# Spreading rows between projection halves, a third early slot, and the second latent layer's first modulation group behind the first expert's gate weights

## The chip, the cores and the metric

One core of one Trainium2 chip runs the kernel; the other cores stand idle. The metric is the device time of one execution in microseconds (us). All arithmetic is float32. Every weight is read once from HBM, 661 MB in all, so two things can set the pace: the rate at which the 16 DMA engines bring weights in, and TensorE (PE), which multiplies them.

## What is computed

Two models follow each other on 256 tokens of width 1024. The first block modulates the normed input (`mod = c @ w_ada + b_ada`), projects it, mixes it by an mLSTM and by a Hyena convolution, projects back, and runs an expert-choice mixture of 16 experts. The second model has two layers. Each of them has its own modulation, mixes the 256 latent tokens and (in layer 0) 256 context tokens by neighbourhood attention, gated linear attention and grouped attention, and ends in a SwiGLU. Cut to what matters here:

```python
def reference(x, c, w_ada, ..., c_2, ctx_2, c_ctx_2, w_ada_2, ...):
    # first block
    mod = (c @ w_ada[0] + b_ada[0])[:, None, :]          # six parts of 1024
    h = rms_norm(x, g_mix) * (1 + sc1) + sh1
    q, k, v, o, gates, hx = jnp.split(h @ w_in + b_in, split_pts, axis=-1)
    x = x + gt1 * (concatenate([mlstm(q, k, v, o, gates), hyena(hx)]) @ w_out)
    hf = rms_norm(x, g_ffn) * (1 + sc2) + sh2
    x = x + gt2 * expert_choice_moe(hf, w_router, w_gate, w_up, w_down)
    x = rms_norm(x, g_final)
    # second model, layers l = 0, 1
    for l in range(2):
        mod, mod_c = silu(c_2) @ w_ada_2[l] + b_ada_2[l], silu(c_ctx_2) @ w_ada_2[l] + b_ada_2[l]
        ...  # mixers, w_out, SwiGLU for latent tokens, and for the context where l == 0
```

The modulation products (`c @ w_ada`) depend on no token. The kernel can therefore place them anywhere before their first use, and the change moves four of them.

## The kernel before, in words

**The weight stream.** Nearly all weights are cut into slots of up to 4096 float32 columns on 128 partitions (2 MiB, "2048 KB" in the profile). The list `stream` holds them in the order in which PE takes them, and SyncE (SP) issues one DMA for each in just that order (`load`, L3110 to L3114). Most slots land in `ring`, which has room for four full slots (16384 columns). A few, named in `early` (L588), land in stretches of `arena` that are dead at that time. Before each DMA, SP waits until PE has finished with the slot `after[n]`, which lay in the same place, or eight slots earlier. SP is in order: while it waits for one slot, all later ones wait too.

**Order of the stream around the change.** After the mixers' projections (z, x1, q, x2, v, o, k) come `out0`, `out1`, then `ada0_7` to `ada0_11` and `ada1_0` to `ada1_3`, and from `n_before` on the experts: `gate0_0` to `gate0_3`, `up0_0` to `up0_3`, and so on, with slots of context weights between them. `ada0_j` are the twelve slots of the modulation of latent layer 0; `ada1_0` to `ada1_3` are the first group of layer 1. Two slots are early ones, `ada0_9` and `ada0_10`. `gate0_0` and `gate0_1` are early ones too; they lie at arena columns 16424 and 20520, and SP waits for `h_ready` 2 (normed tokens of the experts, told by VectorE after L2167) before them.

**Modulation steps.** The list `ADA` gives the steps of the modulation, and `ada(n)` takes the next n of them on PE, ScalarE (ACT) and VectorE (DVE) alike. A "rows" step multiplies one slot (16 matmuls at L1284); four of them fill one PSUM bank, ACT copies it to `row_stage`, and a "turn" step transposes it to columns (8 matmuls in the profile at L1301), which DVE adds to the bias (L1905, L1900). In the kernel before, `ada0_7` to `ada0_10` are taken after the mixers' output (L1551), `ada0_11` after the transposes of the normed tokens (L1564), and `ada(5)` at L1569 takes `ada1_0` to `ada1_3`, with the turns of the groups `ada0_2` and `ada1_0`, while DVE picks the best tokens of each expert (L2186 to L2192).

**Into the experts.** PE then spreads the choice (L1573), gathers the chosen tokens of the first four experts (`tokens_of(0)`, L1583), multiplies the gate slots of expert 0 (L1616), gathers the tokens of the other twelve (`other_tokens`, L1589 to L1599), and goes on with `up0`. ACT copies each gathered bank out. When all of them are copied, SP loads the tables of the second model (L3153 to L3155). From here on, stages of the context's computation stand between the experts' slots.

**The first mixers.** PE projects `x2` in two halves (L1265 by way of `project`), then `token_rows(1, ...)` spreads columns over banks with 16 transposes (L1402), of which DVE takes maxima (L2050 to L2053), then `z_spectrum(0)` (L1418) opens the bank that DVE frees after those maxima (L1900), since banks 0 to 6 are taken in rotation.

## Time and profile before

| | |
|---|---|
| median of 3 runs | 2242.75 us (2240.03 to 2244.28) |
| profiled execution | 2238.4 us, of which the span is 2236.6 us |
| PE busy, loads of weights busy | 1999.5 us (89%), 1406.8 us (63%) |
| DVE, ACT, POOL busy | 588.9, 423.1, 206.4 us |
| DMA | 664.24 MB, mean 297 GB/s |
| mean granted clock of TensorE | 0.964 of full speed |

The profiled execution is 4.35 us shorter than the median. The page's strip of 40 slices (each 55.9 us) shows where each resource is loaded:

```profile
PE   8989998976888898987888887999999999999997
DMA  9938799999999999999999999531587742044450
GB/s 366 374 144 350 297 424 405 422 425 427 389 415 426 427 425 424 422 420 426 425 424 427 419 380 365 138 114 39 180 297 218 187 141 101 15 151 151 127 155 19
```

Each digit is the busy share of a slice in tenths. The first five slices are the mixers of the first block, the sixth to the twenty-fifth hold the experts and the context, and the rest holds the two latent layers.

### The profile page before, as it was taken

How to read it: one execution, taken by the hardware profiler on the slowest of the kernel's cores; microseconds unless marked ns; L12 is line 12 of the kernel's file. 1: busy time of each engine (PE TensorE's matmuls, PEld its weight loads, DVE VectorE, ACT ScalarE, POOL GpSimd, SP SyncE). 2: the span in 40 equal slices, each digit the busy share in tenths (PEclk: the TensorE clock that was granted, in tenths of full speed). 3: DMA queues.
4: the chain of work that ended last, by engine and by line, in shares of the span. 5: the costliest groups of instructions: out<-in, count | busy, mean ns of one | idle time of the engine just before them, and what ended most of it. 6: DMA issues, size and time to landing. Idle time of an engine off the chain costs nothing.

```text
span 2236.6 us, 32618 instructions
## 1 busy us (share of the span) xinstructions
PE 1999.5 (89%) x14110; PEld 1406.8 (63%) x14110; DVE 588.9 (26%) x1168; ACT 423.1 (19%) x776; POOL 206.4 (9%) x183
## 2 busy tenths in 40 slices
PE   8989998976888898987888887999999999999997
PEld 4857575632455466653565543756888877588886
DVE  5655410114412000000002101454432034640001
ACT  3222221211312000000001211434200033630001
POOL 0830000001000000000000000325000003700000
PEclk9999999998998999999999899999999999999999
DMA  9938799999999999999999999531587742044450
GB/s 366 374 144 350 297 424 405 422 425 427 389 415 426 427 425 424 422 420 426 425 424 427 419 380 365 138 114 39 180 297 218 187 141 101 15 151 151 127 155 19
DMA packets 181382, 664.24 MB, mean 297 GB/s; under 512 B 17431, under 2 KB 121400, under 8 KB 142648
## 3 DMA queue, kind: packets, MB, share of 16 engines
q1 hardware_dynamic: 181240, 662.15, 75.7%
q8 instruction: 112, 1.84, 0.3%
q14 instruction: 30, 0.25, 0.0%
HBM read 661.08 MB, written 1.05 MB: 296 GB/s over the span
## 4 chain that ended last, share of the span: by engine, by line
PE 46%; DMA 22%; DVE 4%; ACT 4%; issue 1%; POOL 0%; SPq 0%; ACTq 0%; DVEq 0%; POOLq 0%
PE ps L1177 19%; PE ps L679 9%; DMA ring<-in_context_weights 8%; DMA ring<-in_w_gate 7%; DMA ring<-in_w_down_slots 4%; PE ps L1616 4%; DMA ring<-in_w_up 3%; PE ps L1642 2%; PE ps L1013 2%; PE ps L1186 2%; PE ps L980 2%; ACT arena L2546 1%; PE ps L875 1%; PE ps L705 1%; PE ps L1089 1%
## 5 line engine op out<-in xcount | busy, mean ns | idle before, releaser
L1177 PE MATMUL ps<-arena,ring 128*128 128x256 f32 x1984 | 429.9, 379 | 1.0 <-DVEq L391 0.9
L1177 PEld LDWEIGHTS ps<-arena,ring 128*128 128x128 f32 x1984 | 376.5, 190 | 54.2 <-issue 1.7
L1616 PE MATMUL ps<-ring,arena 128*32 128x256 f32 x4032 | 264.0, 409 | 80.0 <-DMA ring<-in_w_gate 43.7
L679 PE MATMUL ps<-arena,ring 128*128 128x256 f32 (+2 forms) x1372 | 309.7, 386 | 8.6 <-DMA ring<-in_context_weights 8.6
L679 PEld LDWEIGHTS ps<-arena,ring 128*128 128x128 f32 (+2 forms) x1372 | 249.5, 187 | 74.1 <-DMA ring<-in_context_weights 24.4
L1616 PEld LDWEIGHTS ps<-ring,arena 128*32 128x32 f32 x4032 | 127.9, 116 | 200.7 <-DMA ring<-in_w_gate 51.3
L2253 ACT ACTIVATE arena<-ps 128x512 f32<-128x512 f32 (+3 forms) x143 | 76.7, 536 | 738.2 <-PE ps L679 327.8
L1642 PE MATMUL ps<-ring,arena 128*32 128x512 f32 x1024 | 139.1, 668 | 61.1 <-DMA ring<-in_w_down_slots 54.3
L1642 PEld LDWEIGHTS ps<-ring,arena 128*32 128x32 f32 x1024 | 29.8, 117 | 153.0 <-DMA ring<-in_w_down_slots 90.5
L3059 POOL TENSOR_TENSOR XC<-XC,arena 128x256 f32<-128x256 f32 x32 | 23.4, 731 | 989.2 <-ACT XC L2347 968.9
L3069 POOL TENSOR_SCALAR arena<-arena 128x512 f32<-128x512 f32 x48 | 78.4, 1634 | 88.0 <-DVE arena L2964 84.7
L679 PE MATMUL ps<-ring,arena 128*128 128x256 f32 (+3 forms) x312 | 85.7, 426 | 0.0
L1265 PE MATMUL ps<-arena,ring 128*128 128x256 f32 x384 | 84.2, 380 | 1.4 <-ACTq L391 1.4
L2718 DVE SCALAR_TENSOR_TENSOR XC<-ps,arena,XC 128x256 f32<-128x256 f32 x48 | 23.2, 484 | 225.7 <-PE ps L1177 144.2
L980 PE MATMUL ps<-arena,ring 128*128 128x256 f32 x352 | 78.6, 381 | 4.4 <-DMA ring<-in_context_weights 4.4
L1265 PEld LDWEIGHTS ps<-arena,ring 128*128 128x128 f32 x384 | 72.6, 190 | 12.7 <-DVEq L391 2.2
L1873 ACT ACTIVATE arena<-ps 128x256 f32<-128x256 f32 x32 | 12.3, 384 | 352.8 <-PE ps L1616 352.6
L980 PEld LDWEIGHTS ps<-arena,ring 128*128 128x128 f32 x352 | 66.2, 190 | 19.1 <-DMA ring<-in_context_weights 8.9
L679 PEld LDWEIGHTS ps<-ring,arena 128*128 128x128 f32 x312 | 54.5, 190 | 26.9 <-issue 17.1
L3013 DVE TENSOR_TENSOR arena<-arena,ps 128x512 f32<-128x512 f32 x20 | 13.8, 688 | 212.3 <-PE ps L1177 212.3
L2222 DVE TENSOR_TENSOR arena<-arena,ps 128x256 f32<-128x256 f32 x32 | 13.5, 421 | 210.8 <-ACT arena L1873 209.6
L1013 PE MATMUL ps<-arena,ring 128*128 128x258 f32 x224 | 51.0, 381 | 0.0
(374 smaller groups left out, 2015.0 us busy)
## 6 DMA issues: line engine op xcount, KB each, us to landing
ring<-in_w_up SPq DMA_DIRECT2D x64, 2048.0 KB, 13.2
ring<-in_w_down_slots SPq DMA_DIRECT2D x64, 2048.0 KB, 14.2
ring<-in_w_gate SPq DMA_DIRECT2D x62, 2048.0 KB, 13.9
ring<-in_w_ada SPq DMA_DIRECT2D x28, 2048.0 KB, 9.4
ring<-in_w_ffn_in SPq DMA_DIRECT2D x44, 1024.0 KB, 7.7
ring<-in_context_weights SPq DMA_DIRECT2D x35, 1024.0 KB, 14.6
ring<-in_w_ffn_out SPq DMA_DIRECT2D x16, 1408.0 KB, 7.0
ring<-in_w_in SPq DMA_DIRECT2D x9, 2048.0 KB, 11.2
```

Source lines behind the costliest of these rows:

```text
L679: m = mm(o, a, x, start=(k == 0 and r == 0), stop=(k == kt - 1 and last))
L980: m = mm(b[i][:, T * x:T * x + T], w[:, k % 2, c:c + P], HID[:, k, :], start=(k == 0 and x == 0), stop=(k == 21 and x == 1))
L1013: m = mm(b[:, 0:RAW], w[:, k, c:c + P], raw[:, k, :], start=(k == 0), stop=(k == KD - 1))
L1177: m = mm(b, w[:, k, c:c + P], src[:, k, :], start=(k == 0), stop=(k == kt - 1))
L1186: m = mm(b[:, 0:T], held["w"][:, k, c:c + P], oT[X][:, k, :], start=(k == 0), stop=(k == KD - 1))
L1265: m = mm(b[:, T * i:T * i + T], w[:, k, P * (j + i):P * (j + i) + P], src(k), start=(k == 0), stop=(k == ktiles - 1))
L1616: m = mm(b[u][32 * c:32 * c + 32, T * x:T * x + T], xs[:, 2 * h + k, CAP * e:CAP * e + CAP], w[:, k, at_:at_ + T], start=(h == 0 and k == ...
L1642: m = mm(b[a][64 * n + 32 * j:64 * n + 32 * j + 32, :], hdT[:, 2 * a + j, ch, :], w[:, j, at_:at_ + W], start=(i == 0 and odd == 0), stop= ...
L2253: step(a(dst, src, f, **kw), frees=name if frees else None)
L2718: step(stt(out=x, in0=b[:, o:o + T], scalar=mod2[:, l, gate + m, st:st + 1], in1=x, op0=ALU.mult, op1=ALU.add), frees=name if last else None)
L3059: step(nc.gpsimd.tensor_tensor(hat[st][n % 2][:, x, :], ex[st][n % 2][:, x, :], glqk[:, x, :], ALU.mult), lev_ready if x else None)
L3069: step(nc.gpsimd.tensor_scalar(Pr[n % 8], Pr[n % 8], sm[:, n % 8:n % 8 + 1], None, ALU.mult), pn_ready[X])
```

## The change

It has three parts. First, `project("x2")` gets a callback: `token_rows(1, "arow")` is now issued between the two halves of the x2 projection and no longer behind them. Second, `ada0_11` becomes an early slot at arena columns 16424 to 20520, where queries, keys and two of the convolved thirds are dead after the mLSTM weights are made (`p_ready` 1); SP waits for that. Because `gate0_0` lands in the same columns, SP now also waits before `gate0_0` until PE has finished with `ada0_11` (`freed[in_queries]`). Third, `ada1_0` to `ada1_3` leave their place ahead of `n_before` and stand behind `gate0_3` in the stream. PE takes them (`ada(4)`) behind the second half of expert 0's gate, ahead of `other_tokens`, and turns them behind it. ACT and DVE take their steps at matching places.

```diff
--- before.py
+++ after.py
@@ -468,7 +468,7 @@
         for n, count in (("z", 0), ("x1", 0), ("q", 0), ("x2", 1), ("v", 1), ("o", 3), ("k", 4)):
             stream += [(n, cols(w_in, column[n], 512))] + ada_tiles[at_tile:at_tile + count]
             at_tile += count
-        stream += [(f"out{j}", cols(w_out, 512 * j, 512)) for j in range(2)] + ada_tiles[at_tile:]
+        stream += [(f"out{j}", cols(w_out, 512 * j, 512)) for j in range(2)] + ada_tiles[at_tile:24]
 
         SUMMED = 12
         row_buffer = [i % 3 for i in range(SUMMED)]
@@ -557,6 +557,8 @@
                 e = i // 2
                 w = I["w_" + kind][0, e].rearrange("(h p s) n -> p h s n", p=P, s=2)
                 stream += [(f"{kind}{e}_{h}", w[:, h]) for h in (2 * (i % 2), 2 * (i % 2) + 1)]
+            if s == 1:
+                stream += ada_tiles[24:]
             if s in CTX_AT:
                 stream += CTX_STAGES[CTX_AT[s]][1]
         n_moe = len(stream)
@@ -585,8 +587,10 @@
         NU, NP = len(UNITS2), len(HEADS2)
 
 
-        early = {n_before: 16424, n_before + 1: 20520, n_before + 6: 12312}
-        early |= {n: {"ada0_9": 5120, "ada0_10": 0}[name] for n, (name, _) in enumerate(stream) if name in ("ada0_9", "ada0_10")}
+        early = {n_before: 16424, n_before + 1: 20520, n_before + 10: 12312}
+        dead = {"ada0_9": 5120, "ada0_10": 0, "ada0_11": 16424}
+        early |= {n: dead[name] for n, (name, _) in enumerate(stream) if name in dead}
+        in_queries = [name for name, _ in stream].index("ada0_11")
         landing, count = [], [0] * LANES
         place_of, after = [], []
         top = 0
@@ -618,10 +622,10 @@
         ADA = [[("rows", "ada", j)] for j in range(4)] + [[("turn", "ada", 0)], [("sum", "ada", 1)], [("turn", "ada", 1)], [("sum", "ada", 2)]]
         ADA += [[("rows", "ada", 10)], [("rows", "ada", 11)]]
         ADA_GROUPS = [("ada", j) for j in range(3)] + [("ada0_", j) for j in range(3)] + [("ada1_", 0)]
-        for g in range(3, 7):
+        for g in range(3, 6):
             name, j = ADA_GROUPS[g]
             ADA += [[("rows", name, 4 * j), ("turn", *ADA_GROUPS[g - 1])]] + [[("rows", name, 4 * j + h)] for h in range(1, 4)]
-        ADA += [[("turn", "ada1_", 0)]]
+        ADA += [[("turn", "ada0_", 2)]] + [[("rows", "ada1_", h)] for h in range(4)] + [[("turn", "ada1_", 0)]]
         LATE = {n: name for n, (name, _) in enumerate(stream) if name[:4] == "late"}
         late_sum, late_row = at(24064, 2048), at(26112, W)
         GROUP = {"ada": 0, "ada0_": 3, "ada1_": 6}
@@ -1296,7 +1300,7 @@
                 n = 1 if name == "ada" else 2
                 turned[0] += 1
                 pe.wait_ge(row_ready, turned[0])
-                b = open_bank(pe, f"col_{name}{j}", MIX_BANKS)
+                b = open_bank(pe, f"col_{name}{j}", CTX_BANKS if name == "ada1_" else MIX_BANKS)
                 for i in range(4):
                     m = mm(b[:, 4 * n * i:4 * n * i + 4 * n], stage_of(name, j)[:, P * i:P * i + P], tb("pick")[:, 0:8:3 - n], start=True, stop=True)
                 close_bank(m, f"col_{name}{j}")
@@ -1369,10 +1373,12 @@
             T1v = T1.rearrange("p (a b) -> p a b", b=T)
 
 
-            def project(n):
+            def project(n, between=None):
                 w = take(n)
                 for i in range(2):
                     fmajor(f"{n}{i}", w, 2 * i, lambda k: hT[:, k, :])
+                    if i == 0 and between is not None:
+                        between()
                 release_with(f"{n}1")
 
             def by_groups(name, w):
@@ -1452,8 +1458,7 @@
             close_bank(m, "F")
             z_by_token(0)
             ada()
-            project("x2")
-            token_rows(1, "arow")
+            project("x2", between=lambda: token_rows(1, "arow"))
             z_spectrum(0)
             ada(2)
             w = take("v")
@@ -1566,7 +1571,7 @@
             for t in range(TT):
                 m = nc.tensor.transpose(b[0:NE, P * t:P * t + P], aff[:, t, :], ident)
             close_bank(m, "affT")
-            ada(5)
+            ada()
             pe.wait_ge(best_ready, 1)
             for i in range(2):
                 b = open_bank(pe, f"best{i}", MIX_BANKS)
@@ -1665,7 +1670,9 @@
                         gu = [open_bank(pe, f"gu{e}{u}", EXPERT_BANKS) for u in range(2)]
                     expert("gate", i, gu)
                     if i == 1:
+                        ada(4)
                         other_tokens()
+                        ada()
                     if g and i % UNITS < 4:
                         combine(g - 1, i % UNITS, TURN_BANKS)
                 elif kind == "up":
@@ -1852,7 +1859,7 @@
                     b = read_bank(act, f"ht{t}{half}")
                     step(a(htok[:, t, 512 * half:512 * half + 512], b[:], ACT.Copy), frees=f"ht{t}{half}")
                     tell(ht_ready)
-            ada(6)
+            ada(2)
             def tokens_of(g):
                 for half in range(2):
                     b = read_bank(act, f"xs{g}{half}")
@@ -1860,6 +1867,7 @@
                     tell(xs_ready)
 
             tokens_of(0)
+            ada(4)
             for g in range(1, GROUPS):
                 tokens_of(g)
             for g2 in range(2):
@@ -2191,7 +2199,7 @@
             for i in range(2):
                 step(tt(own[e16, i, :].rearrange("p (e s) -> p e s", s=CAP), bc(best[e16, i, :], 1, NE, CAP), bc(ident[e16, 0:NE], 2, NE, CAP), ALU.mult))
             tell(best_ready)
-            ada(5)
+            ada()
             which = read_bank(dve, "best0")
             for t in range(TT):
                 step(ts(sel[:, t].rearrange("p e s -> p (e s)"), which[:], tb("token")[:, t:t + 1], None, ALU.is_equal), frees="best0" if t else None)
@@ -2209,6 +2217,7 @@
                     if sem:
                         tell(sem)
 
+            ada(5)
             dve.wait_ge(s_x, 32)
             dve.wait_ge(xs_ready, 8)
             dve.wait_ge(ct_ready, 2)
@@ -3137,6 +3146,8 @@
                     sp.wait_ge(y_ready, 2)
                 if stream[n][0] == "ada0_10":
                     read_bank(sp, "num111")
+                if stream[n][0] == "ada0_11":
+                    sp.wait_ge(p_ready, 1)
                 load(n)
                 for i in rows_behind.get(stream[n][0], ()):
                     load_row(i)
@@ -3145,9 +3156,10 @@
             for n in range(n_before, len(stream)):
                 if n == n_before:
                     sp.wait_ge(h_ready, 2)
-                if n == n_before + 6:
+                    sp.wait_ge(*freed[in_queries])
+                if n == n_before + 10:
                     sp.wait_ge(ht_ready, 4)
-                if n == n_before + 9:
+                if n == n_before + 13:
                     sp.wait_ge(xs_ready, 8)
                     sp.wait_ge(ct_ready, 2)
                     sp.dma_start(arena[:, 0:n_tab2], I["tables2"]).then_inc(s_tab2, 16)
```

## Rows read from the trace of the kernel before

**Rows 1.** Windows: stretch, length, busy us by engine, PEclk, DMA share, GB/s.
```profile
0.00:260.00 260.00, 243.98 (x1206) 167.58 (x1210) 150.51 (x262) 66.55 (x117) 66.77 (x65) 0.97 0.78 301
260.00:400.00 140.00, 123.26 (x1138) 82.06 (x1130) 19.23 (x55) 27.38 (x45) 0.00 (x0) 0.93 0.99 410
400.00:540.00 140.00, 110.00 (x1351) 62.02 (x1348) 31.47 (x68) 26.44 (x42) 11.81 (x16) 0.94 1.00 423
...
1580.00:1810.00 230.00, 229.88 (x1078) 200.47 (x1077) 61.22 (x73) 20.69 (x35) 3.65 (x5) 1.00 0.72 224
```

**Rows 2.** Waits of PE from 300 to 600 us: total, times, longest.
```profile
PE ps L1616 <- DMA ring<-in_w_gate: 10.4, 6, 3.8
```

**Rows 3.** Timeline of SP's queue: start, length, line, what it issues.
```profile
209.47 3.11 SPq L3114 DMA_DIRECT2D ring<-in_w_ada  x2
212.70 7.03 SPq L3114 DMA_DIRECT2D arena<-in_w_ada  x2
241.46 24.92 SPq L3114 DMA_DIRECT2D ring<-in_w_ada  x5
266.43 0.47 SPq L3144 DMA_DIRECT2D XC<-in_ctxT  x1
266.99 3.58 SPq L3114 DMA_DIRECT2D arena<-in_w_gate  x2
...
313.09 0.33 SPq L3153 DMA_DIRECT2D arena<-in_tables  x1
```

**Rows 4.** Windows in the front and of two gaps among the experts, columns as before.
```profile
230.00:240.00 10.00, 10.00 (x48) 8.79 (x48) 1.32 (x3) 0.63 (x1) 0.00 (x0) 1.00 0.14 57
241.00:244.80 3.80, 3.80 (x20) 3.33 (x19) 0.97 (x2) 0.63 (x1) 0.00 (x0) 1.00 0.62 183
244.80:316.60 71.80, 64.80 (x577) 42.97 (x576) 20.09 (x54) 20.69 (x36) 0.00 (x0) 0.93 0.97 396
600.00:610.00 10.00, 9.54 (x84) 5.48 (x84) 2.59 (x6) 2.34 (x7) 0.00 (x0) 0.83 0.80 301
1300.00:1320.00 20.00, 20.00 (x117) 10.06 (x112) 1.75 (x1) 0.47 (x1) 0.00 (x0) 0.91 0.82 315
```

**Rows 5.** Timeline of PE in the first mixers, with idle time and its releaser.
```profile
94.10 14.06 PE L1265 MATMUL ps<-arena,ring 128*128 128x256 f32 x64
108.00 1.91 PE L1402 MATMUL ps<-tab,arena 128*128 128x128 f32 x16
117.99 5.95 PE L1418 MATMUL ps<-arena,tab 128*128 128x512 f32 x8 [8.08 <-DVE arena L1900]
...
172.34 3.70 PE L1418 MATMUL ps<-arena,tab 128*128 128x512 f32 x8
```

**Rows 6.** Timeline of DVE around them, and its writing of the normed tokens.
```profile
98.53 5.28 DVE L1986 SCALAR_TENSOR_TENSOR arena<-arena,par 128x2048 f32<-128x2048 f32 x2
108.70 0.69 DVE L2050 TENSOR_REDUCE arena<-ps 128x4 f32<-128x512 f32 x1 [4.89 <-PE ps L1402]
117.67 0.17 DVE L1900 TENSOR_TENSOR arena<-ps,par 128x16 f32<-128x16 f32 x1
...
254.31 4.13 DVE L2167 SCALAR_TENSOR_TENSOR arena<-XC,arena 128x256 f32<-128x256 f32 x8
```

**Rows 7.** Timeline of PE from the slot ada0_11 to the first up slots.
```profile
264.03 1.92 PE L1284 MATMUL ps<-ring,arena 128*32 128x512 f32 x16
...
283.77 6.72 PE L1583 MATMUL ps<-arena 128*128 128x128 f32 x32 [0.95 <-issue]
291.22 3.66 PE L1616 MATMUL ps<-arena 128*32 128x256 f32 x64 [0.73 <-issue]
...
299.33 11.57 PE L1583 MATMUL ps<-arena 128*128 128x128 f32 x96
310.74 1.04 PE L1598 MATMUL ps<-tab,arena 128*128 128x128 f32 x8
311.71 3.66 PE L1616 MATMUL ps<-ring,arena 128*32 128x256 f32 x64
```

## Prediction, made before the changed kernel was run

> **What bounds the kernel now.** I read the windows first, because the bound changes by stage. Up to 260 us PE is busy 244 of 260 us and DMA has holes (share 0.78). From 260 us on DMA is full: its share is 0.99 to 400 us and 1.00 with 423 GB/s to 540 us, while PE idles 30 us of 140. In the latent layers PE is busy 229.88 of 230 us [rows 1]. The page's strip shows the same nine tenths or more up to about 1370 us. PE waits for gate slots there, for instance 10.4 us in six places [rows 2]. So the experts' stretch ends when a fixed number of bytes has arrived, and nothing in it can be made up by PE. An idle us of DMA ahead of that stretch moves the end by one us; an idle us of PE there costs something only if it delays a DMA. I therefore read next what SP issued and when [rows 3], and the windows beside it.
>
> The reader is to see one hole. `ada0_7` to `ada0_10` are issued from 209.47 to 219.7 us; the next issue is at 241.46 us [rows 3]. In between the DMA share falls to 0.14 [rows 4]. The issue at 241.46 is `ada0_11`, which waits for the ring place of `out0`. Behind it everything flows: `ada1_0` to `ada1_3`, the last at about 266.0 us when PE ends `ada0_11` (264.03 + 1.92) [rows 7], then the context tokens at 266.43 and `gate0_0` at 266.99 [rows 3].
>
> **A clock for DMA.** A full slot is 2.097 MB, 4.96 us at 423 GB/s [rows 1]. The windows give 183 x 3.8 = 0.70 MB to 244.8 us and 396 x 71.8 = 28.43 MB from there to 316.6 us, 29.13 MB in all [rows 4]. That is just five modulation slots, four gate and four up slots (13 x 2.097 = 27.26 MB), the context tokens (1.05) and one context slot of 1600 columns (0.82). So before the change `up0_3` has fully arrived at 316.6 us, and it is my mark, since the bytes behind it are the same in both kernels. The 0.70 MB are 1.64 us of full rate, so the flow starts in effect at 244.8 - 1.64 = 243.2 us, 1.7 us after its issue at 241.46. At full rate the rest would take 67.2 us; it took 71.8. Those 4.6 us are small holes, one of them around the late last slot at 266 us.
>
> **Part 1, rows between the halves of x2.** It removes nothing; 16 transposes move. PE now does 7.0 us of x2 from 94.10 (half of 14.06), the transposes (1.91) to 103.1, and the second half to 110.1 us [rows 5]. DVE's row sums end at 98.53 + 5.28 = 103.81 us; it then waited 4.89 us for the transposes [rows 6]. Now it starts at 103.9. From its first maximum to the end of L1900 it needs 117.84 - 108.70 = 9.1 us [rows 6], so the bank is free at 113.0 and not 117.9. `z_spectrum` starts at 113.1 and not 117.99: **4.9 us gained**, and of 8.08 us of idle PE about 3.0 stay [rows 5]. The slot of x2 is freed 2 us later (110.1), so `o` is issued 2 us later; it is taken over 30 us on, which hides it. Could the gain be larger? `z_spectrum` took 5.95 us after the 8 us of idle and 3.70 us in its second use [rows 5], so up to 2.25 us more come back if the clock stays up over a pause of 3 us. I take none of it and keep it as a bound. Could it be nothing? If ACT or POOL were late next, yes; PE idles nowhere else for them up to 218 us, so I keep 0 only as the other bound. The transfers up to `ada0_10` are each issued on an event of PE or DVE, so they shift by the same 4.9 us.
>
> **Part 2, the early slot.** `ada0_11` no longer waits for `out0` but for `p_ready` 1, which PE's numerators wait for as well, and `ada0_10` ahead of it waits for the last numerator. So it is issued right behind `ada0_10`, at 219.7 - 4.9 = 214.8 us, and the context tokens behind it. This fills the hole with 4.96 + 2.48 = 7.4 us of work for DMA. In exchange `gate0_0` waits until PE has ended `ada0_11`. PE takes that slot at the same place in its program, so this is 265.95 - 4.9 = **261.05 us**. `h_ready` 2 is out by 254.31 + 4.13 - 4.9 = 253.5 [rows 6] and not the last. All else that SP could load, `gate0_1` to `gate0_3` and the rest, is queued behind this wait, though ring places come free from `out1` on. DMA has nothing from about 234 us (the four slots ended near 232 before [rows 4], so 227 now, plus 7.4) to 262.8. The hole grows from 11 us to 28.
>
> **Part 3, layer 1's group moved.** The four slots, 19.8 us of DMA time, were what DMA did from 246 to 266 us, in a stretch where gates could not be loaded; now they stand behind the gates, in the full stretch. The four "rows" steps (4 x 1.92 = 7.7 us) and a turn (about 1.05) leave PE ahead of the gates and come in behind them. Best tokens are then waited for by PE for DVE alone, as before. PE goes from `ada0_11` at 261.0 to `tokens_of(0)` at about 272, to `gate0_0` at about 280 instead of 291.2 [rows 7]. That gain is not kept: `ada1_3` is the eighth slot after the wait and lands at 262.8 + 8 x 4.96 = 302.5, or some 303.3 with its completion. Its rows end at 305.2, `other_tokens` (11.57 + 1.04) at 317.8, the turn at 318.9. `up0_0` then starts 7.2 us later than the 311.71 of before [rows 7]. The tables were issued 1.3 us after the last transposes [rows 3, 7], now at 319.1, while DMA still has slots to bring; no new hole there. The bank of the turn comes from the context's four and the rotation moves by one; each is freed by an ACT copy of 0.6 us, and I cost that at nothing.
>
> **The sum.** From the wait to my mark are 4 gates, 4 modulation and 4 up slots and the context slot, 12 x 2.097 + 0.82 = 25.98 MB, 61.4 us at 423 GB/s. They start in effect at 261.05 + 1.7 = 262.8 and end at 324.2 us, against 316.6: **+7.6 us**. Behind the mark I worked the ring places out by the rule of `after`: 31 slots, the last in the second group's down part, wait for another slot than before, mostly by one place, some earlier and some later; I cost that at nothing while DMA is full, and the gaps' loss bounds it. PE waits for DMA in both, so the delay stays to the end of the experts, and the latent layers have the same work. The profiled execution would be 2238.4 + 7.6 = 2246.0; the median, 4.35 us above it, 2242.75 + 7.6 = **2250.4 us**. Bounds: 2.25 less by the clock (+5.3), 4.6 more if the new flow has as many small holes as the old (+12.2), 4.9 more if part 1 gives nothing (+12.5; both together +17.1).
>
> One price differs by page. The row says 423 GB/s [rows 1]. The Trainium skill, page "DMA: Bandwidth & Descriptors", section Specifications, gives an HBM limit of about 358 GB/s per core. By that the 25.98 MB would take 72.6 us, an estimate, and the delay would be larger by some 11 us; the trace does not agree, with 423 GB/s over 140 us, and it decides.
>
> **Rivals.**
> *The delay is taken up on the way* (within 0.2%). DMA has gaps among the experts, 301 GB/s from 600 to 610 us (2.9 us lost) and 315 from 1300 to 1320 us (5.1 us lost) [rows 4]. If those gaps came from a computation that runs on its own time, a later stream would fill them, and 7.6 - 2.9 - 5.1 is about 0: 2242 to 2246. For it: PE is busy 9.54 of 10 and 20 of 20 us there [rows 4]. Against it: ahead of these places PE waits for slots, so its work there is late by as much as the slots.
>
> *PE, not DMA, sets the pace up to 540 us* (the other side, faster). A full DMA could merely be running ahead. Then PE has `up0_0` at: `gate0_0` 279.7, gates 7.7, rows 7.7, gather 12.6, turn 1.05, that is 308.8, 2.9 us earlier than 311.71 [rows 7]; with the 2.25 us of clock it gains 5.2 us, 2237.6. It decides if every slot behind the gates has landed when PE asks. Against it stand the 10.4 us of waits for gates [rows 2] and PE's 30 idle us of 140 [rows 1]. The Trainium skill, page "Perfetto Trace Analysis", section Optimization Strategy, says that a kernel whose most-contended engine changes over time may gain by interleaving the regimes; by that rule PE work moved from the mixers into the DMA-bound experts should pay, which is this rival. The rows agree that there are two regimes, but the bytes moved with the work.
>
> *Part 1 does not do what it says*: a second wait (POOL's convolution, or the bank of the second half) holds PE until 118. Then the wait for `ada0_11` ends at 265.95 and the sum is +12.5, 2255.3. Against it: nothing but DVE releases PE in that place [rows 5].
>
> **How the numbers follow.** A measurement of this kernel tells about 0.2% (4.5 us) from no change. The forecast, held gates with +5.3 to +9.5 (2248.0 to 2252.3), gets 0.48; more holes or no gain in part 1 (+9.5 to +17, to 2259.8) 0.20; the delay taken up (2239 to 2247) 0.20; faster 0.12. Slower is then 0.48 + 0.20 = 0.68 (all but a sliver of these lie above 2247.2), less 0.01 for that sliver: 0.67; within 0.2% 0.21; faster 0.12. The range must leave out no more than 0.2: from 2239.0, which leaves out most of the faster case (0.11), to 2257.0, which cuts the top of the holes' case (0.05).
>
> **What would show it.** In the trace after: PE's idle ahead of L1418 about 3 us, its start at about 113; the issue of `ada0_11` near 215 us; no issue of SP from about 216 to 261 us, with a DMA share near nothing from 235 to 261; `gate0_0` at 261; `gate0_0` multiplied near 280, `ada1_3` not before 303; full DMA behind it and each later issue about 7 to 8 us later, up to the last down slots. I am wrong if SP issues a gate slot before 255 us, if DMA in the later gaps loses clearly less than before, or if the start of `up0_0` is earlier than 311.7.

## The result, and the profile after

The changed kernel takes 2254.18 us (median of 4 runs, 2252.07 to 2257.05) against 2241.39 us (4 runs) of the kernel before: 12.8 us more, ratio 1.006 with a 95% interval of 1.0043 to 1.0077. I had forecast 2250.4 us, slower, with a range of 2239 to 2257. Direction and range held. The cost is 5 us larger than the sum's 7.6; the time is only 3.8 us above the forecast, because the kernel before measured 1.4 us less than the median that I had added the sum to.

The profiled execution has a span of 2250.3 us, 13.7 us above the 2236.6 of before. First, SP's queue in the changed kernel (start, length, line, what it issues):

```profile
206.63 7.54 SPq L3123 DMA_DIRECT2D arena<-in_w_ada  x3
214.23 0.46 SPq L3155 DMA_DIRECT2D XC<-in_ctxT  x1
259.98 0.82 SPq L3123 DMA_DIRECT2D arena<-in_w_gate  x2
260.85 1.15 SPq L3123 DMA_DIRECT2D ring<-in_w_gate  x2
262.04 24.11 SPq L3123 DMA_DIRECT2D ring<-in_w_ada  x4
...
320.72 0.33 SPq L3165 DMA_DIRECT2D arena<-in_tables  x1
```

Where before had an issue at 241.46 and a full queue behind it [rows 3], nothing is issued here from 214.7 to 259.98 us. Then four gate slots go out within 2 us; the places of the two ring slots among them had been free since PE ended the products with `out0` (e5 below issues into that place at 235.25 us) and with `out1` (at about 242.3 us in this trace). The windows of the same stretch (columns as in rows 1) show what DMA does meanwhile:

```profile
220.00:230.00 10.00, 10.00 (x52) 8.78 (x51) 3.21 (x9) 0.00 (x0) 0.00 (x0) 1.00 1.02 424
230.00:240.00 10.00, 10.00 (x48) 8.79 (x47) 2.90 (x6) 1.26 (x2) 0.00 (x0) 1.00 0.40 137
240.00:250.00 10.00, 9.19 (x59) 5.62 (x57) 4.54 (x8) 3.47 (x7) 0.00 (x0) 1.00 0.00 1
250.00:260.00 10.00, 9.88 (x96) 4.98 (x92) 3.51 (x13) 5.33 (x10) 0.00 (x0) 1.00 0.01 2
260.00:270.00 10.00, 3.99 (x12) 2.71 (x13) 7.49 (x25) 2.48 (x5) 0.00 (x0) 0.62 0.92 357
```

PE's timeline from the first mixers and from the gates on:

```profile
101.37 1.91 PE L1408 MATMUL ps<-tab,arena 128*128 128x128 f32 x16
103.11 7.07 PE L1269 MATMUL ps<-arena,ring 128*128 128x256 f32 x32
112.75 5.12 PE L1424 MATMUL ps<-arena,tab 128*128 128x512 f32 x8 [2.56 <-DVE arena L1908]
...
278.61 3.66 PE L1621 MATMUL ps<-arena 128*32 128x256 f32 x64 [0.69 <-ACT arena L1866]
282.09 3.64 PE L1621 MATMUL ps<-ring,arena 128*32 128x256 f32 x64
288.37 1.92 PE L1288 MATMUL ps<-ring,arena 128*32 128x512 f32 x16 [2.65 <-DMA ring<-in_w_ada]
293.35 3.50 PE L1288 MATMUL ps<-ring,arena 128*32 128x512 f32 x16 [3.06 <-DMA ring<-in_w_ada]
298.30 1.92 PE L1288 MATMUL ps<-ring,arena 128*32 128x512 f32 x16 [1.45 <-DMA ring<-in_w_ada]
303.48 3.56 PE L1288 MATMUL ps<-ring,arena 128*32 128x512 f32 x16 [3.26 <-DMA ring<-in_w_ada]
306.97 11.57 PE L1588 MATMUL ps<-arena 128*128 128x128 f32 x96
...
320.14 3.66 PE L1621 MATMUL ps<-ring,arena 128*32 128x256 f32 x64
```

The first spectrum (L1424) starts at 112.75 us instead of 117.99 [rows 5]. PE reaches the first gate slot 12.6 us earlier than before and `up0_0` 8.4 us later [rows 7], with 10.4 us of waiting for the four modulation slots in between.

**The lag by bytes.** To follow it to the end I summed the rates of the windows of 10 us from 0 on and read off when each kernel had moved the same number of MB. 101.3 MB are the mark of the prediction: in the kernel before they are reached at 316.7 us. As the end of the experts I take the start of the last combination on PE (16 matmuls at L1655, L1660 after the change).

```
                 101.3 MB   125 MB   220 MB   end of experts   span
before             316.7     372.6    600.7      1380.4       2236.6
changed kernel     322.7     381.4    610.9      1390.4       2250.3
lag                 +6.0      +8.8    +10.2        +9.9        +13.7
```

So the lag has three parts: 6.0 us are there at the mark, 4 us arise behind it among the experts, and 3.7 us in the latent layers. Of the last part 3.5 us arise in one place, the start of layer 1. There PE computes the gate ranks (16 matmuls). PE's timeline in the kernel before:

```profile
1817.92 3.65 PE L1013 MATMUL ps<-arena,ring 128*128 128x258 f32 x16
1821.86 4.96 PE L700 MATMUL ps<-arena,ring 128*32 128x256 f32 x16 [0.29 <-ACT arena L2256]
1827.53 7.17 PE L705 MATMUL ps<-arena,ring 128*128 128x256 f32 x32 [0.70 <-DVE arena L2752]
```

and DVE's, the row that frees the bank of the second raw query:

```profile
1827.12 0.36 DVE L2752 TENSOR_SCALAR arena<-arena,ps 128x256 f32<-128x256 f32 x1
```

The same place in the changed kernel, PE:

```profile
1828.14 3.65 PE L1017 MATMUL ps<-arena,ring 128*128 128x258 f32 x16
1837.80 1.93 PE L704 MATMUL ps<-arena,ring 128*32 128x256 f32 x16 [6.00 <-DVE arena L2761]
1839.66 8.72 PE L709 MATMUL ps<-arena,ring 128*128 128x256 f32 x32
```

and DVE:

```profile
1837.34 0.36 DVE L2761 TENSOR_SCALAR arena<-arena,ps 128x256 f32<-128x256 f32 x1
```

The two DVE rows are 10.22 us apart, like the rows of PE ahead of them. Before, PE did not need that bank and had followed ACT's tiles one by one from 1821.86 on. Now it stands until 1837.34 + 0.36 = 1837.70 and starts at 1837.80. That is 5.7 us more of lag. The product then takes 1.93 us instead of 4.96, since it no longer follows ACT, and the wait of 0.70 us behind it is gone, which gives 3.8 us back. The next product takes 8.72 instead of 7.17 us, with a mean granted clock of 0.82 from 1839.6 to 1848.3 us and of 1.00 in the same place before, 1.55 us more. Together the lag grows from 10.2 to 13.7 us. The order in which banks are opened says why: in the kernel before `gl_lrx1` opens bank 7, in the changed one bank 4, which `rq1x1`, the second raw query, holds. The latent layers share one rotation over banks 4 to 7 with the context, and the moved turn of `ada1_0` takes one place in it. In layer 0 the gate ranks move from bank 4 to bank 5 by the same step; the wait there is 4.93 us instead of 4.03.

### The profile page after: what moved, and what is told of

Read it like the earlier page. It is cut to its first block, busy times and chain, and to the rows that moved or that the text cites. A ratio compares the mean times of both kernels' runs of the same rounds, so it can differ in the third digit from the quotient of the medians.

```text
span 2250.3 us, 32619 instructions
## 1 busy us (share of the span) xinstructions
PE 2004.7 (89%) x14110; PEld 1407.0 (63%) x14110; DVE 591.4 (26%) x1168; ACT 423.1 (19%) x776; POOL 206.4 (9%) x183
## 4 chain that ended last, share of the span: by engine, by line
PE 47%; DMA 22%; DVE 4%; ACT 3%; issue 1%; ACTq 0%; POOL 0%; SPq 0%; DVEq 0%; POOLq 0%
PE ps L1181 19%; PE ps L683 10%; DMA ring<-in_w_gate 7%; DMA ring<-in_w_down_slots 6%; DMA ring<-in_context_weights 5%; PE ps L1621 4%; DMA ring<-in_w_up 4%; PE ps L1647 2%; PE ps L1017 2%; PE ps L1190 2%; PE ps L984 2%; ACT arena L2555 1%; PE ps L879 1%; PE ps L709 1%; PE ps L845 1%
## 5 line engine op out<-in xcount | busy, mean ns | idle before, releaser
L1647 PE MATMUL ps<-ring,arena 128*32 128x512 f32 x1024 | 141.9, 683 | 59.0 <-DMA ring<-in_w_down_slots 53.0
L1288 PE MATMUL ps<-ring,arena 128*32 128x512 f32 x304 | 42.5, 689 | 13.4 <-DMA ring<-in_w_ada 12.6
## 6 DMA issues: line engine op xcount, KB each, us to landing
ring<-in_w_gate SPq DMA_DIRECT2D x62, 2048.0 KB, 13.3
```

The costliest lines, as they stand in the source:

```text
L1288: m = mm(row_bank[0][32 * g:32 * g + 32, :], cpad[:, 2 * h + k, :], w[:, k, W * g:W * g + W], start=(h == 0 and k == 0), stop=(h == 3 and ...
L1647: m = mm(b[a][64 * n + 32 * j:64 * n + 32 * j + 32, :], hdT[:, 2 * a + j, ch, :], w[:, j, at_:at_ + W], start=(i == 0 and odd == 0), stop= ...
```

## The experiments

Theory H: an empty DMA queue costs its length, since DMA is full from there to the end of the experts; the wait of `gate0_0` for `ada0_11` empties it. Theory B: the 3.5 us at layer 1 are the shifted rotation of banks. Rivals: part 3 costs by PE's late start of `up0_0`; the slot in the dead columns costs by itself; there is slack behind the front.

**e1_rows_alone**, the kernel before with part 1 only:

```diff
-            project("x2")
-            token_rows(1, "arow")
+            project("x2", between=lambda: token_rows(1, "arow"))
```

> The kernel before with the first part alone: the transposes of the first maxima stand between the halves of the x2 projection. In the changed kernel PE's first spectrum started at 112.75 instead of 117.99 us and took 5.12 instead of 5.95, and everything on PE up to 240 us came 6.07 us earlier. Theory (the gain of part 1 is real and reaches the end, since it shifts the start of the full DMA stretch): each issue from 120 us on about 6 us earlier, the last down slots as well, total 6 us less than before (ratio 0.997). Rival (what ends the experts does not hang on the front): the front 6 us earlier and the total within 1 us of before.

Measured: 2235.1 us (11 runs) against 2240.84, ratio 0.9976 (0.9965 to 0.9988). The mark is reached at 310.6 us, 6.1 earlier than in the kernel before; the experts end at 1376.4 us, 4.1 earlier in this profile, and the median is 5.7 us lower. Part 1 is a gain of 4 to 6 us that reaches the end, and the rival of slack falls.

**e2_rows_behind**, the changed kernel with the same lines undone.

> The changed kernel with its first part undone. Theory: the wait of gate0_0 for the slot ada0_11 ends at about 266 instead of 259.98 us, all later issues are 6 us later than in the changed kernel, and the total is some 6 us above it, 19 us above before (ratio 1.0085). Rival (the first part costs or gives nothing at the end): the changed kernel's time, ratio 1.006.

Measured: 2262.17 us (4 runs), ratio 1.0092 (1.0074 to 1.011), 8.0 us above the changed kernel's median. `gate0_0` was issued at 264.13 us and the mark reached at 326.9, each 4.2 later than in the changed kernel. I had expected 266 us and 6 us. The direction follows the theory, the size is not settled: the profiled span, 2253.7 us, is only 3.4 us above the changed kernel's, while the medians of 4 runs each are 8.0 apart.

**e3_group_ahead**, parts 1 and 2 without part 3:

```diff
         stream += [(f"out{j}", cols(w_out, 512 * j, 512)) for j in range(2)] + ada_tiles[at_tile:]
...
-        early |= {n: {"ada0_9": 5120, "ada0_10": 0}[name] for n, (name, _) in enumerate(stream) if name in ("ada0_9", "ada0_10")}
+        dead = {"ada0_9": 5120, "ada0_10": 0, "ada0_11": 16424}
+        early |= {n: dead[name] for n, (name, _) in enumerate(stream) if name in dead}
...
                     sp.wait_ge(h_ready, 2)
+                    sp.wait_ge(*freed[in_queries])
```

> Parts 1 and 2 without part 3: rows between the halves, ada0_11 early in the dead columns, gate0_0 still waits for it, but ada1_0 to ada1_3 stay ahead of the gates and can fill the time of that wait from the ring. Theory (what costs is an empty DMA queue between 235 and 260 us, not the wait as such): ada1_0 to ada1_3 are issued at about 235.4, 242, 248 and 250 us, gate0_0 at 260, up0_3 has arrived at about 303 instead of 322.7, then DMA has some 5 us of nothing until the chosen tokens are copied and the tables may be loaded at about 308; total 7 to 12 us below before (ratio 0.995 to 0.997). Rival (the early slot itself, with the wait in front of gate0_0, costs): the total above that of the first part alone, ratio near 1.000.

Measured: 2232.27 us (5 runs), ratio 0.9957 (0.9942 to 0.9973): 8.6 us below before and the fastest of all. The hold of `gate0_0` is in this kernel too, but SP has something to issue ahead of it:

```profile
205.85 7.54 SPq L3117 DMA_DIRECT2D arena<-in_w_ada  x3
234.61 15.33 SPq L3117 DMA_DIRECT2D ring<-in_w_ada  x4
249.99 0.47 SPq L3149 DMA_DIRECT2D XC<-in_ctxT  x1
259.19 0.82 SPq L3117 DMA_DIRECT2D arena<-in_w_gate  x2
```

and DMA is full through the hold (windows, last columns DMA share and GB/s):

```profile
245.00:250.00 5.00, 4.19 (x37) 1.33 (x33) 4.16 (x6) 2.96 (x6) 0.00 (x0) 1.00 1.00 392
250.00:255.00 5.00, 5.00 (x54) 2.01 (x54) 1.82 (x6) 2.17 (x5) 0.00 (x0) 1.00 1.02 424
255.00:260.00 5.00, 4.48 (x38) 2.52 (x38) 1.18 (x7) 3.07 (x5) 0.00 (x0) 1.00 1.00 399
...
300.00:305.00 5.00, 5.00 (x62) 4.14 (x65) 0.28 (x2) 2.39 (x4) 0.00 (x0) 1.00 0.54 229
305.00:310.00 5.00, 5.00 (x51) 3.41 (x44) 0.07 (x1) 4.60 (x8) 0.00 (x0) 1.00 0.88 285
```

The mark is reached at 304.3 us. As expected some gain is given back right behind it, where DMA is at 229 and 285 GB/s because the tables wait for the copied tokens (issued at 304.62). So the early slot and the wait are no cost by themselves: with them this kernel is even 2.8 us below e1, which has part 1 alone (2235.1 us).

**e5_no_hold**, parts 1 and 3 without part 2 (`ada0_11` back in the ring, no wait of `gate0_0` for it):

```diff
-        dead = {"ada0_9": 5120, "ada0_10": 0, "ada0_11": 16424}
+        dead = {"ada0_9": 5120, "ada0_10": 0}
...
                     sp.wait_ge(h_ready, 2)
-                    sp.wait_ge(*freed[in_queries])
```

> Parts 1 and 3 without part 2: ada0_11 lands in the ring again behind out0, so gate0_0 waits for the normed tokens only and not for PE's use of ada0_11. Theory (the hold of gate0_0 costs its length): gate0_0 is issued at about 252.4 instead of 259.98 us, up0_3 has arrived at about 315.5 instead of 322.7, the total is 7 us below the changed kernel, 5 to 6 us above before (the shift of banks is still in; ratio 1.0025). Rival (the four modulation slots behind the gates cost, whatever the wait): still 2254, ratio 1.006.

Measured: 2247.05 us (11 runs), ratio 1.0033 (1.0021 to 1.0045), 7.1 below the changed kernel's median. SP's queue, and a window of 5 us:

```profile
235.25 0.37 SPq L3122 DMA_DIRECT2D ring<-in_w_ada  x1
...
252.30 0.82 SPq L3122 DMA_DIRECT2D arena<-in_w_gate  x2
```

```profile
245.00:250.00 5.00, 4.19 (x35) 1.09 (x33) 3.56 (x5) 2.36 (x5) 0.00 (x0) 1.00 0.01 3
```

It stays slower than before although part 1 is in it, since DMA still had nothing to do from 245 us to the issue at 252.30. The mark comes at 317.8 us, 4.9 earlier than in the changed kernel and not 7.2 as expected. Part of the difference lies from 280 to 290 us: DMA moved 311 and then 339 GB/s in windows of 5 us, some 2.3 us of full rate lost, while SP waited for PE to free places in the ring.

Four kernels with part 1 in them now separate the other two parts (medians in us):

```
                     part 2 out          part 2 in
part 3 out     e1    2235.10       e3    2232.27
part 3 in      e5    2247.05       after 2254.18
```

Part 3 costs 12 us by itself and 22 us beside the hold; the hold costs nothing where the four modulation slots stand ahead of it, and 7 us where they do not. Each figure is good to some 3 us; by the ratios, each to the kernel before as measured beside it, they are 13, 23, none and 6. So the cost is not the hold alone. Part 3 took away what the queue could issue (an empty stretch of some 7 us is left even in e5, and the banks of theory B add theirs), and part 2 made the empty stretch longer.

**e9_taken_early** and **e10_longer_hold** change the length of the hold. In e9 PE takes `ada0_11` before the logits, which also makes the logits later:

```diff
             close_bank(m, "ss1")
-            ada(4)
+            ada(5)
...
                     close_bank(m, f"ht{t}{half}")
-            ada()
```

> The changed kernel, and PE takes ada0_11 right behind ada0_10, ahead of the logits: the hold of gate0_0 ends at about 256.5 instead of 259.98 us. Theory (each us of hold is a us at the end, for DMA has nothing from 235 on): gate0_0 issued 3.1 to 3.8 us earlier, total some 3 us less than the changed kernel, about 2251, ratio 1.0045. Rival (the hold is not what costs): unchanged, 1.006.

and in e10 SP waits longer:

```diff
                     sp.wait_ge(*freed[in_queries])
+                    sp.wait_ge(best_ready, 1)
```

> The changed kernel, and SP waits ahead of gate0_0 also until the best tokens are chosen (DVE tells it at 268.2 us in the changed kernel), 8.3 us longer. Theory (each us of hold is a us at the end): total about 8 us above the changed kernel, 2262, ratio 1.0095. Rival (some slack lies between the gates' arrival and the end of the experts, since PE multiplies the first gate slot only at 278.6 us): the gates would land at 276 and be taken nearly as before; total within 3 us of the changed kernel, ratio 1.006 to 1.0075.

Measured: e9 2252.18 us (6 runs), ratio 1.005 (1.0033 to 1.0066), a step in the expected direction that its interval does not separate from the changed kernel; e10 2262.48 us (6 runs), ratio 1.009 (1.0073 to 1.0108), 8.3 us above it, as theory H has it. In one table, by the issue of `gate0_0` in each profile (in e2 and e5 it is not the hold alone that differs: the whole front is later in e2, and e5 has no hold):

```
kernel            gate0_0 issued   mark    end of experts   ratio to before
e5_no_hold            252.30      317.8       1384.8          1.0033
e9_taken_early        256.78      319.9       1388.0          1.005
changed kernel        259.98      322.7       1390.4          1.006
e2_rows_behind        264.13      326.9       1391.7          1.0092
e10_longer_hold       268.39      331.1       1397.4          1.009
```

An issue 16.1 us later moves the mark by 13.3 us and the end of the experts by 12.5 us. From the changed kernel to e10 it is one to one at the mark (8.4 and 8.4 us, 7.0 at the end of the experts); from e5 to the changed kernel 7.7 us of delay are 4.9 at the mark. In e9 PE multiplies the first gate slot at 281.31 us, 2.7 later than in the changed kernel, and the experts end 2.4 us earlier all the same. In e10 the gates came so late that PE waited for them (a row of PE's timeline there), which the changed kernel's PE did not:

```profile
287.10 3.64 PE L1621 MATMUL ps<-ring,arena 128*32 128x256 f32 x32 [3.81 <-DMA ring<-in_w_gate]
```

but the hold had its price already below that point. There it is the stream that is late, not the gate.

**e6_tokens_first**, the changed kernel with the other tokens gathered ahead of the four modulation slots (ACT's copies in the same order):

```diff
                     if i == 1:
-                        ada(4)
                         other_tokens()
+                        ada(4)
                         ada()
```

> The changed kernel, but PE gathers the tokens of the other twelve experts ahead of ada1_0 to ada1_3 and not behind them, so that it does not stand idle for those slots (10.4 us of waits in four places) with 11.6 us of gathering still to do. Theory (DMA sets the pace, and the late gathering costs only the small holes between 320 and 350 us): up0_0 at about 307 instead of 320.14, tables issued at about 301, the loss of those holes, 2 to 3 us, comes back, total 2251 to 2252. Rival (PE's late start of up0_0 is the cost of the change): the total 8 us or more below the changed kernel, 2246 or less.

Measured: 2252.56 us (6 runs), ratio 1.0046 (1.0033 to 1.0059). The tables went out at 308.32 and PE was ready for `up0_0` at 309.6, but it had to wait for the slot:

```profile
300.76 7.07 PE L1288 MATMUL ps<-ring,arena 128*32 128x512 f32 x64 [1.33 <-ACT arena L1873]
308.59 1.06 PE L1305 MATMUL ps<-tab,arena 128*128 128x8 f32 x8 [0.75 <-ACTq L391]
312.36 3.20 PE L1621 MATMUL ps<-ring,arena 128*32 128x256 f32 x32 [2.71 <-DMA ring<-in_w_up]
```

PE could have started `up0_0` 10.5 us earlier than in the changed kernel and did so 7.8 us earlier, and the median fell by 1.6 us, less than the intervals tell apart. I had expected `up0_0` at 307 and the tables at 301. The rival in its full size, that PE's late start is the cost (8 us or more), falls. But the order also has a price: the ring places are freed later, `up0_0` is issued at 302.74 instead of 290.35, and the mark comes at 326.3 us, 3.6 later than in the changed kernel. A smaller gain by PE's earlier start could hide behind that; e6 does not exclude it.

**e4_latent_banks** sets the rotation back where the latent layers begin, **e7_all_banks** right behind the moved turn:

```diff
                 N, bk = f"x{l}", MAIN_BANKS
+                if l == 0:
+                    turn_of[MAIN_BANKS] -= 1
```

```diff
                 close_bank(m, f"col_{name}{j}")
+                if name == "ada1_":
+                    turn_of[CTX_BANKS] -= 1
```

> The changed kernel, with the rotation over PSUM banks 4 to 7 set back by one where latent layer 0 begins, so that the latent layers use the banks of the kernel before; nothing else differs. In the changed kernel the first projection of layer 1 (16 matmuls of the gate ranks) waited 6.00 us until DVE had read the second raw query's bank, and the lag behind the kernel before grew from 10.2 to 13.7 us there. Theory (the moved turn shifted the rotation, and this projection now opens the bank of the second raw query, 4, instead of bank 7): that wait is gone, the lag stays at about 10.2 us to the end, total 3 to 4 us less than the changed kernel (about 2250.5; ratio 1.004). Rival (it is the clock or the order of DMAs there): the wait stays, total 2254, ratio 1.006.

> The changed kernel with the rotation over banks 4 to 7 set back right behind the moved turn, so that context and latent layers both use the banks of the kernel before. Theory: as with the latent layers alone, about 2250.5; the context's stages run beside a full DMA and a bank more or less costs them nothing. Rival (part of the lag's growth from 6 us at the mark to 10 us at 600 us comes from the context's banks): the lag at 600 us is 3 us smaller and the total 2247.

Measured: e4 2249.39 us (6 runs), ratio 1.0038 (1.0024 to 1.0052); e7 2250.22 us (7 runs), ratio 1.0031 (1.0015 to 1.0047). Their medians are 4 to 5 us below the changed kernel's, with intervals that overlap its own, so the traces have to decide. The wait is gone in e4:

```profile
1825.93 3.65 PE L1017 MATMUL ps<-arena,ring 128*128 128x258 f32 x16
1829.87 4.96 PE L704 MATMUL ps<-arena,ring 128*32 128x256 f32 x16 [0.29 <-ACT arena L2267]
```

From the end of L1017 to this start are 0.29 us, as before the change, and not 6.00. From the last combination to the end of the span there are 855.8 to 856.2 us in the six profiles with the old rotation in the latent layers (before, e1, e3, e4, e7, e8), 859.9 in the changed kernel, and 862.0 to 862.7 in the other five with the shifted one (e2, e5, e6, e9, e10). No profile lies between. Theory B holds, and the shift costs 3.7 us in the changed kernel's profile and about 6 in the others; most of the difference arises early in latent layer 0, where for instance the product behind the wait took 7.66 us in the changed kernel and 9.01 in e9. The context's banks add nothing that shows: e7 and e4 differ by less than their intervals, and 220 MB are reached in e7 at 613.3 us, not earlier than the 610.9 of the changed kernel.

**e8_ahead_taken_early** joins e3 and e9, in search of a faster kernel.

> As e3_group_ahead, and PE takes ada0_11 right behind ada0_10, ahead of the logits, so that the wait of gate0_0 ends at about 256 instead of 259.2 us. Theory (an empty DMA queue costs its length): DMA has its last issue at 250 and runs dry near 258, so about 3 us of hole close; but in that kernel a second hole, 300 to 309 us (the tables wait for the copied tokens), is set by PE and the choice of tokens, which now comes 1.9 us later, so at the end 0 to 2 us either way against e3_group_ahead: ratio 0.995 to 0.997. Rival (the wait itself is what costs): 3 us less than e3_group_ahead, 0.9945.

Measured: 2239.1 us (12 runs), ratio 0.9985 (0.9972 to 0.9998), some 7 us above e3. That is a miss: both theories had it within 3 us of e3. The tables were issued at 310.22 us instead of 304.62, and DMA stood nearly still before them:

```profile
305.00:310.00 5.00, 5.00 (x58) 4.40 (x61) 0.00 (x0) 2.28 (x4) 0.00 (x0) 1.00 0.29 121
```

The product with `ada0_11` filled a wait of PE for the affinities; taken earlier it delays them, and PE waited 2.27 us for them where e3 waited 0.41 (first e3, then e8):

```profile
259.51 0.39 PE L1570 MATMUL ps<-tab,arena 128*16 128x128 f32 x2 [0.41 <-DVEq L391]
```

```profile
262.85 0.39 PE L1569 MATMUL ps<-tab,arena 128*16 128x128 f32 x2 [2.27 <-DVEq L391]
```

Part of the rest is the front of that profile, whose spectrum began 1.6 us later than e3's. How the whole 7 us divide was not tried.

## Why the prediction was right, and where it was short

- *The bound.* Right. DMA from the wait to the experts' end sets that stretch: in the table of holds 16.1 us of delay are 12.5 at the end of the experts.
- *Part 1, 4.9 us.* The mechanism was right (DVE frees the bank at 112.7, PE idles 2.56 us instead of 8.08). The term was 6.07 us, 5.24 from the earlier start and 0.83 because the spectrum took 5.12 us and not 5.95, inside the bound of 2.25 for the clock. It reached the end in e1 (4.0 us in the profiles, 5.7 by the medians).
- *Part 2, the hold.* Right in its steps: `ada0_11` out just ahead of the context tokens at 214.23 (forecast 214.8), nothing behind it until 259.98 (261.05), and DMA at 1 to 2 GB/s from 240 us on. e5 and e10 show that its length costs; e9 alone would not. That it costs only together with part 3 is what e3 shows; the prediction had said both halves (that nothing behind the wait could be issued, and that the four slots "were what DMA did from 246 to 266 us") without separating their prices.
- *Part 3.* `gate0_0` multiplied at 278.6 (forecast 280), `up0_0` at 320.14 (318.9). The 1.2 us come from the last row product, which took 3.56 us instead of 1.92 behind a wait of 3.26 (granted clock 0.53 from 303.4 to 307.0 us); the turn and the gathering were a little shorter than in the sum. I had costed it at full speed. The other slow product, at 293.35, cost nothing, since PE waits for the next slot anyway.
- *The mark.* Forecast 324.2 us against 316.6, +7.6; measured 322.7 against 316.7, +6.0. Of the difference of 1.6 us, 1.2 are part 1's larger gain.
- *"PE waits for DMA in both, so the delay stays to the end of the experts."* This step was short by 4 us. 2.8 of them arise between 101.3 and 125 MB: in windows of 5 us DMA moves 373 to 397 GB/s from 325 to 345 us, where the kernel before has 415 to 446 from 320 to 345. I had noted PE's late start of `up0_0` and seen "no new hole there". The runs show how near the hole was. The table sets the margin (start of `up0_0` on PE before the mark is reached) beside what each kernel lost against the kernel before between the two byte counts:

```
kernel            up0_0    mark   margin   loss to 125 MB
before            311.7    316.7    5.0        0
e1_rows_alone     305.9    310.6    4.7       +0.2
e10_longer_hold   326.8    331.1    4.3       +0.3
e2_rows_behind    322.6    326.9    4.3       +0.6
e4_latent_banks   321.3    324.2    2.9       +2.0
e7_all_banks      320.9    323.5    2.6       +3.6
changed kernel    320.1    322.7    2.6       +2.8
e9_taken_early    317.4    319.9    2.5       +3.2
e5_no_hold        315.8    317.8    2.0       +2.6
e3_group_ahead    303.3    304.3    1.0       +4.6
e8                308.9    309.6    0.7       +4.5
```

  With more than 4 us of margin 0.6 us or less is lost, with 3 or less 2 to 5 us are. e6, where `up0_0` starts 14 us ahead of the mark, loses 0.7. The likely reading is that what SP issues next (the tables, and the slots whose places PE's `up` products free) comes too late for a full queue; the table shows that the loss goes with the margin, and no run separates the tables from the places. What I left out is that this margin was 5.0 us before the change, and that the gathering (12.6 us) behind the last modulation slot leaves about half of it. About 1 us more arises up to 220 MB and was not explained.
- *The banks: "the rotation moves by one; each is freed by an ACT copy of 0.6 us, and I cost that at nothing."* This step failed. It cost 3.7 us in the profile and 4 to 5 us by the medians of e4 and e7, not in the context, where I had looked at it, but in the latent layers, for the most part 1500 us later at the start of layer 1, where the bank is held by a raw query that DVE frees.
- *The rivals.* The delay was not taken up in the gaps at 600 and 1300 us: they are there in both kernels and wander with the stream (303 GB/s from 610 to 620 us now, 301 from 600 to 610 before [rows 4]). PE does not set the pace up to 540 us: e6 gave it 7.8 us and the median fell by 1.6. As e6's stream was 3.6 us later at the mark, that excludes a cost of 8 us, not one of a few. Part 1 did what it says. The Trainium skill, page "Perfetto Trace Analysis", section Optimization Strategy, says that interleaving regimes may improve performance. The runs show a limit of that: e3, which left the modulation's bytes where DMA had room, gains 8.6 us; e5, which moved bytes and products into the full stretch, is 12 us slower than e1, which did not. The runs do not bear it out for work that brings its bytes along.

The measured 12.8 us are then, by the profile's 13.7: 6 at the mark (the sum's 12.5 without part 1, less the 6.1 that part 1 gave, and 0.4 of rest), 4 behind it and 3.7 from the banks.

That the range held was in part luck. 2254.18 us lies where I had placed "more holes or no gain in part 1". Neither came about: up to the mark the new flow has no such holes, and part 1 gave more than I had counted. What lifted the time was 7.7 us in two places that I had costed at nothing, and the bound was wide enough for them by accident.

## What to carry to other kernels

Where one in-order queue feeds a DMA that is full further on, as in this kernel, a transfer's wait delays everything behind it, and costs what the queue could otherwise have moved: before adding one, list what the queue could still issue during that time, and put the transfers whose places are free ahead of the wait, as e3 does. Moving the products of a load into a DMA-bound stretch gains nothing if the load moves with them. And an operation that takes a place in a round-robin of buffers shifts every later user of it; look at where a later user meets a buffer that is freed late, or set the rotation back.

## What the runs showed of the hardware

How much a short idle time of PE costs beyond its own length differed from run to run. The first spectrum (8 matmuls of 512 columns) took 3.7 us in the five profiles in which PE had idled 0.5 to 1.5 us ahead of it (e3, e4, e6, e8, e9), 5.1 to 6.5 us in those with 2.6 to 3.2 us (the changed kernel, e1, e5, e7, e10), and 6.0 and 6.2 us in the two with 8.08 us (the kernel before, e2). But of the row products in e10 one took 1.92 us and the next 3.53, behind 3.04 and 3.05 us of idle. The mean granted clock of the changed kernel is 0.83 from 110 to 120 us and 0.83 from 290 to 310 us, where such slow stretches lie, and 1.00 in the 10 us on either side of each. So a saving of idle can be worth more than its length, as part 1's was, and a sum like mine should carry it as a bound on both sides, for added waits too.
